# The opening modulation computed by quarters instead of by halves

## The reference, cut to what matters

```python
cond = jax.nn.silu(c)                                   # c: (1, 1024)
mod = (cond @ ada_w[0] + ada_b[0])[:, None, :]          # ada_w[0]: (1024, 6144)
sh1, sc1, g1, sh2, sc2, g2 = jnp.split(mod, 6, axis=-1)
h = rmsnorm(x, norm1_g[0]) * (1 + sc1) + sh1            # x: (1, 256, 1024)
proj = h @ w_in[0] + b_in[0]
```

## Time and profile before

| | us |
|---|---|
| three runs | 1454.43, 1455.65, 1456.05 (median 1455.65) |
| the profiled execution | 1453.79 |
| its span in the trace | 1452.0 |
| PE busy in the span | 1430.3 |
| POOL busy | 1211.7 |
| ACT busy | 756.5 |
| DVE busy | 722.8 |

### The profile page before, as it was taken

One profiled execution on the slowest core, in us unless ns is written; L12 is line 12 of the kernel. 1 busy time (PEld: TensorE's weight loads), 2 busy tenths in 40 slices (PEclk: granted clock), 3 DMA queues, 4 the chain that ended last, 5 costly groups with the idle time before them and its releaser, 6 DMA issues.

```text
span 1452.0 us, 21556 instructions
## 1 busy us (share of the span) xinstructions
PE 1430.3 (99%) x7600; PEld 1199.9 (83%) x7600; DVE 722.8 (50%) x1556; ACT 756.5 (52%) x1275; POOL 1211.7 (83%) x986
## 2 busy tenths in 40 slices
PE   7999999999999999999999999999999999999997
PEld 5898777799988987778888888878888888788886
DVE  7863654766643754754566303454650044655202
ACT  4435775644445345765644445574654345655442
POOL 3899989898888987559898897967999977789995
PEclk9999999999999999999999999999999999999999
DMA  9994557688975986337676565643656656446651
GB/s 361 402 357 159 192 170 227 232 305 314 315 263 161 399 314 219 110 102 232 216 244 205 185 206 164 191 154 131 191 201 196 221 163 188 132 163 200 195 199 56
DMA packets 149559, 313.35 MB, mean 216 GB/s; under 512 B 10934, under 2 KB 31818, under 8 KB 149451
## 3 DMA queue, kind: packets, MB, share of 16 engines
q1 hardware_dynamic: 147696, 310.62, 63.6%
q10 hardware_dynamic: 1756, 1.35, 0.3%
HBM read 310.87 MB, written 1.06 MB: 215 GB/s over the span
## 4 chain that ended last, share of the span: by engine, by line
PE 92%; DVE 4%; ACT 2%; POOL 1%; DMA 1%; issue 1%; SPq 0%; POOLq 0%; DVEq 0%; ACTq 0%
PE bank L814 58%; PE bank L859 12%; PE bank L860 8%; PE bank L857 5%; PE bank L1022 1%; PE bank L1006 1%; POOL lo_units L751 1%; PE bank L895 1%; PE bank L992 1%; DMA x_rows<-in_x 1%; PE bank L1109 1%; PE bank L1038 1%; PE bank L1074 1%; ACT hi_units L1402 1%; PE bank L1064 0%
## 5 line engine op out<-in xcount | busy, mean ns | idle before, releaser
L751 POOL TENSOR_TENSOR lo_units<-raw_units,hi_units 128x512 fp32r<-128x512 f32 (+3 forms) x928 | 1151.5, 1276 | 219.2 <-ACT hi_units L1402 218.0
L1402 ACT ACTIVATE hi_units<-raw_units 128x1024 fp32r<-128x1024 f32 (+1 forms) x470 | 482.7, 1030 | 410.9 <-PE bank L814 248.4
L814 PE MATMUL bank<-hi_units,turned 128*128 128x512 f32 (+3 forms) x1600 | 441.2, 390 | 1.7 <-DVE turned L1940 0.8
L814 PEld LDWEIGHTS bank<-hi_units,turned 128*128 128x128 f32 x1600 | 291.6, 189 | 53.3 <-DVE turned L1940 2.8
L860 PE MATMUL bank<-turned,lo_units 128*128 128x256 f32 x1024 | 288.0, 281 | 0.0
L814 PE MATMUL bank<-hi_units,turned_wide 128*128 128x512 f32 x992 | 274.6, 391 | 0.0
L859 PE MATMUL bank<-turned,hi_units 128*128 128x512 f32 x736 | 259.2, 397 | 0.0
L814 PE MATMUL bank<-lo_units,turned 128*128 128x512 f32 (+3 forms) x800 | 252.7, 383 | 0.8 <-POOL lo_units L751 0.5
L814 PEld LDWEIGHTS bank<-hi_units,turned_wide 128*128 128x128 f32 x992 | 185.3, 188 | 38.5 <-issue 0.5
L860 PEld LDWEIGHTS bank<-turned,lo_units 128*128 128x128 f32 x1024 | 194.3, 190 | 0.2
L814 PEld LDWEIGHTS bank<-lo_units,turned 128*128 128x128 f32 x800 | 149.7, 188 | 30.6 <-POOL lo_units L751 3.6
(11 more groups left out here) (266 smaller groups left out, 1290.9 us busy)
## 6 DMA issues: line engine op xcount, KB each, us to landing
ada_units<-in_ada_w SPq DMA_DIRECT2D x88, 512.0 KB, 7.7
raw_units<-in_w_ffn_tiles SPq DMA_DIRECT2D x72, 512.0 KB, 5.5
raw_units<-in_mlp_w_out SPq DMA_DIRECT2D x64, 512.0 KB, 3.3
raw_units<-in_mlp_w_tiles SPq DMA_DIRECT2D x56, 512.0 KB, 3.3
raw_units<-in_w_in SPq DMA_DIRECT2D x56, 458.0 KB, 9.8
raw_units<-in_w_in SPq DMA_DIRECT2D x48, 512.0 KB, 6.8
raw_units<-in_w_ffn_out SPq DMA_DIRECT2D x44, 512.0 KB, 3.5
raw_units<-in_moba_w_qkv SPq DMA_DIRECT2D x24, 512.0 KB, 3.7
```

What stands on the lines that cost most here:

```text
L751: pool.tensor_tensor(LO[:, s, b, 0:w], RAW[:, u["slot"], b, 0:w], HI_[:, s, b, 0:w].bitcast(F32), ALU.subtract).then_inc(lo_ready.sem, lo_ ...
L814: ins = pe.matmul(BANK[2 * c["pair"] + t][:, 0:w], (A[a] if A is BT else A[:, a])[:, part, t * P:(t + 1) * P], W[:, s, b, 0:w], start=(i = ...
L1402: act.activation(HI_[:, s, 0:n, 0:w], RAW[:, u["slot"], 0:n, 0:w], ACT.Copy)\
```

## The change

The host rearranges the first 2048 columns of `ada_w[0]` that are wanted into four quarters of 512: 256 columns of scale and the 256 of shift that belong to the same two tiles of h. Bias and gain come as columns from the host too (`first_columns`), in one small transfer on ACT's queue, so the two products that turned rows into columns are gone, and so are the memsets of `FIRST`. PE, ACT and DVE now work by quarter: sums of a quarter, its two operations for scale and shift on DVE, the application to one group of h on ACT (both tiles), rounded copy, remainder, and then unit q of c0 and unit q of c1. The last ada unit of quarters 0 and 3 is multiplied by PE, (0, 0, 3) and (0, 3, 3). The transfers of c and of the constants move from SPq to ACT's queue, x comes after two ada units instead of five, and weight units are mixed in among the ada units. `tables()` and `angles()` stand behind the fourth quarter, as they stood behind the second half. ACT rounds weight units only behind each quarter's copy.

```diff
-FIRST_BANK = {(0, 2): 0, (0, 0): 0, (0, 3): 0, (0, 1): 0}
-PE_UNITS = {(0, 3, 1)}
+N_FIRST = 4
+PE_UNITS = {(0, 0, 3), (0, 3, 3)}
+FIRST_BANK = {(0, q): 0 for q in range(N_FIRST)}
...
-    scale0, shift0, scale1, shift1 = first = [ada(0, c) for c in (2, 0, 3, 1)]
+    first = [ada(0, q) for q in range(N_FIRST)]
     chunks.extend(first)
-    stream.extend(scale0["units"] + shift0["units"])
+    sums = [u for c in first for u in c["units"]]
...
+            behind = {4: (c0, 0), 5: (c1, 0), 8: (c0, 1), 9: (c1, 1), 12: (c0, 2), 13: (c1, 2)}
+            for n, u in enumerate(sums):
+                stream.append(u)
+                if n in behind:
+                    c, i = behind[n]
+                    stream.append(c["units"][i])
+            stream.extend((c0["units"][3], c1["units"][3], vec(*vec0), vec(*vec1)))
...
-        sp.dma_start(COND, dram["c"].rearrange("b (p k) -> (b p) k", p=P)).then_inc(c_in, 16)
-        sp.dma_start(CON[:, 0:n_early], dram["constants"][:, 0:n_early]).then_inc(const_in, 16)
...
-                if (l, c, i) == (0, 0, 1):
+                if (l, c, i) == (0, 0, 2):
                     for t in range(NT):
                         sp.dma_start(X[:, t, :], dram["x"][0, t * P:(t + 1) * P, :]).then_inc(x_in[t], 16)
-                src = dram["ada_w"][l].rearrange("(p k) n -> p k n", p=P)[:, i * UNIT_K:(i + 1) * UNIT_K, c * CW:(c + 1) * CW]
+                if (l, c) in FIRST_BANK:
+                    src = dram["ada_first"][c][:, i * UNIT_K:(i + 1) * UNIT_K, :]
+                else:
+                    src = dram["ada_w"][l].rearrange("(p k) n -> p k n", p=P)[:, i * UNIT_K:(i + 1) * UNIT_K, c * CW:(c + 1) * CW]
...
+        def column_sums(q):
+
+            u = quarters[q]["units"][-1]
+            shared = (0, q, u["i"]) in PE_UNITS
+            pe.wait_ge(ada_used.sem, ada_used.at(quarters[q]["units"][-2 if shared else -1]["index"]))
             for j in range(4):
-                at = (KT if n >= 2 else 0) + 4 * half + j
-                pe.matmul(columns[:, at:at + 1], FIRST[0:1, n * CW + j * P:n * CW + (j + 1) * P], ONES[0:1, 0:1], start=False, stop=False)
-
-        def column_products(c, i):
-
-            u = c["units"][i]
-            at = (KT if c["key"][2] >= 2 else 0) + 4 * (c["key"][2] % 2)
-            pe.wait_ge(ada_in[u["home"]][u["slot"]], 16 * (u["turn"] + 1))
+                ins = pe.matmul(columns[:, 4 * q + j:4 * q + j + 1], MOD[:, q * CW + j * P:q * CW + (j + 1) * P], ONES[:, 0:1],
+                                start=j == 0, stop=j == 3 and not shared)
+            if not shared:
+                ins.then_inc(product.sem, product.mark(("columns", q)))
+                return
+            pe.wait_ge(ada_in[u["home"]][u["slot"]], 16)
             for k in range(UNIT_K):
                 for j in range(4):
-                    ins = pe.matmul(columns[:, at + j:at + j + 1], ada_raw(u)[:, k, j * P:(j + 1) * P], COND[:, i * UNIT_K + k:i * UNIT_K + k + 1],
-                                    start=False, stop=False)
+                    ins = pe.matmul(columns[:, 4 * q + j:4 * q + j + 1], ada_raw(u)[:, k, j * P:(j + 1) * P],
+                                    COND[:, KT - UNIT_K + k:KT - UNIT_K + k + 1], start=False, stop=(k, j) == (UNIT_K - 1, 3))
             ins.then_inc(ada_multiplied.sem, ada_multiplied.mark(u["index"]))
 
...
+        def keep_running(n, bank):
 
             for _ in range(n):
-                pe.matmul(BANK[3][:, :], con("ident"), ada_raw(scale0["units"][0])[:, 0, :], start=True, stop=True)
-
-        pe.wait_ge(ada_in[scale0["units"][0]["home"]][scale0["units"][0]["slot"]], 16)
-        keep_running(1)
-        pe.wait_ge(first_gain_in, 16)
-        gain_columns(0)
-        pe.wait_ge(first_bias_in, 16)
-        bias_columns(scale0)
-        keep_running(2)
-        column_sums(scale0)
+                pe.matmul(bank[:, :], con("ident"), ada_raw(quarters[0]["units"][0])[:, 0, :], start=True, stop=True)
+
+        first_unit = quarters[0]["units"][0]
+        pe.wait_ge(ada_in[first_unit["home"]][first_unit["slot"]], 16)
+        keep_running(4, BANK[3])
...
-                keep_running(1)
-                column_sums(shift0)
-                keep_running(2)
-                for i in (0, 1):
-                    pe.wait_ge(turned_lo.sem, turned_lo.at((tag, i)))
-                    unit(c0, i, HT)
-                turn(tag, O, range(4), 2, ready)
-                turn(tag, O, range(4), 3, ready)
-                pe.wait_ge(rows.sem, rows.at(("columns", 0)))
-                gain_columns(1)
-                column_products(scale1, 1)
-                unit(c1, 0, HT)
-                column_sums(scale1)
-                column_sums(shift1)
-                unit(c1, 1, HT)
-                for c in (c0, c1):
-                    for i in (2, 3):
-                        pe.wait_ge(turned_lo.sem, turned_lo.at((tag, i)))
-                        unit(c, i, HT)
+                keep_running(1, BANK[3])
+                column_sums(0)
+                keep_running(1, BANK[3])
+                for q in range(N_FIRST):
+                    pe.wait_ge(turned_lo.sem, turned_lo.at((tag, q)))
+                    unit(c0, q, HT)
+                    if q + 2 < N_FIRST:
+                        turn(tag, O, range(4), q + 2, ready)
+                    unit(c1, q, HT)
+                    if q + 1 < N_FIRST:
+                        column_sums(q + 1)
...
+        def first_hi(q):
+
+            act.wait_ge(rows.sem, rows.at(("columns", q)))
+            act.wait_ge(turned.sem, turned.at((("n1", 0), q)))
+            bank = BANK[(TQ, TP)[q % 2]]
+            for k in (0, 1):
+                part = bank[:, k * S:(k + 1) * S]
+                ins = act.activation(part, part, ACT.Identity, scale=GAINED[:, 2 * q + k:2 * q + k + 1], bias=BIASED[:, 4 * q + 2 + k:4 * q + 3 + k])
+            ins.then_inc(act_side.sem, act_side.mark(("whole", q)))
+            act.wait_ge(act_side.sem, act_side.at(("whole", q)))
+            act.activation(HT[:, 2 * q:2 * q + 2, 0, :], bank[:, :].rearrange("p (k s) -> p k s", k=2), ACT.Copy)\
+                .then_inc(turned_hi.sem, turned_hi.mark((("n1", 0), q)))
 
...
+        act.dma_start(COND, dram["c"].rearrange("b (p k) -> (b p) k", p=P)).then_inc(c_in, 16)
+        act.dma_start(CON[:, 0:n_early], dram["constants"][:, 0:n_early]).then_inc(const_in, 16)
+        act.wait_ge(c_in, 16)
+        act.activation(CT, COND, ACT.Tanh, scale=0.5).then_inc(act_side.sem, act_side.mark("cond"))
+        act.dma_start(NM[:, 0:3 * KT], dram["first_columns"]).then_inc(first_in, 16)
...
-        prep(2)
         for l in range(DEPTH):
             if l == 0:
-                first_hi(0)
-                prep(NH)
-                first_hi(1)
-                prep(NH + 3)
+                for q in range(N_FIRST):
+                    if q == N_FIRST - 1:
+                        prep(2 * q + 1)
+                    first_hi(q)
+                    prep(2 * q + 2)
...
+        def first_sum(q, kt):
+
+            u = by_key["ada", 0, q]["units"][kt // UNIT_K]
+            if (0, q, u["i"]) in PE_UNITS:
+                return
+            part, partial = ada_raw(u)[:, kt % UNIT_K, :], BANK[SB_[0]][:, :]
+            if kt % UNIT_K == 0:
+                dve.wait_ge(ada_in[u["home"]][u["slot"]], 16)
+                ada_done[0] += 1
+            if kt == 0:
+                ins = v.tensor_scalar(partial, part, COND[:, kt:kt + 1], None, ALU.mult)
+            else:
+                n = KT - (UNIT_K if (0, q, KT // UNIT_K - 1) in PE_UNITS else 0)
+                total = MOD[:, q * CW:(q + 1) * CW] if kt == n - 1 else partial
+                ins = v.scalar_tensor_tensor(total, part, COND[:, kt:kt + 1], partial, ALU.mult, ALU.add)
+            if kt % UNIT_K:
+                tell(ins, ada_used, u["index"])
+            else:
+                link(ins)
+
+        def first_columns(q):
+
+            dve.wait_ge(first_in, 16)
+            last = by_key["ada", 0, q]["units"][-1]
+            if (0, q, last["i"]) in PE_UNITS:
+                dve.wait_ge(ada_multiplied.sem, ada_multiplied.at(last["index"]))
+            else:
+                dve.wait_ge(product.sem, product.at(("columns", q)))
+            cols = slice(4 * q, 4 * q + 4)
+            link(v.tensor_tensor(BIASED[:, cols], BANK[SB_[1]][:, cols], FIRST_BIAS[:, cols], ALU.add))
+            say(v.scalar_tensor_tensor(GAINED[:, 2 * q:2 * q + 2], BIASED[:, 4 * q:4 * q + 2], 1.0, FIRST_GAIN[:, 2 * q:2 * q + 2], ALU.add, ALU.mult),
+                ("columns", q))
 
...
-        sums_upto(5)
+        for kt in range(4):
+            first_sum(0, kt)
         dve.wait_ge(act_side.sem, act_side.at(("root", ("n1", 0))))
         say(v.reciprocal(RR[:, 0:NT], RSTD), "inverse root")
-        sums_upto(8)
+        for kt in range(4, KT):
+            first_sum(0, kt)
         for l in range(DEPTH):
             if l == 0:
-                first_columns(0)
-                sums_upto(15)
```

(67 more changed lines are left out.)

42 lines of the change are left out of this document (2 added, 40 removed).

## The result

The changed kernel takes 1466.07 us (median of six runs, 1463.90 to 1467.73), the kernel before 1455.80: the ratio is 1.0068 with a 95% interval of 1.0056 to 1.0079, some 10 us slower. The profiled execution took 1467.73, with a span of 1465.9. The forecast was 1463.9 in a range of 1459.8 to 1469.5. Quarters are numbered 0 to 3 here, so the fourth quarter is quarter 3.

What follows compares the result with a forecast made beforehand. PE was taken to bound the kernel, so an opening delay reaches the end nearly whole. Unit 8 6.7 us later plus 1.5 for the clock is 8.2, on 1455.65: 1463.9 us, range 1459.8 to 1469.5.

Steps and rivals of the forecast that it cites:

- Rival (b): The delay is absorbed behind the opening, the transfers setting the pace: about 1455 us; chance 0.07.
- Start of the work: Opening: ada units issued 0.9 us earlier and x there at 9.3, so PE's first unit starts at 20.8, 4.0 earlier.
- The boundaries: Between quarters: nothing covers the chain from column sums to remainder, so PE idles 3.04 us, three times.
- Rival (c): Quarter boundaries: the chain behind the sums is covered, unit 8 starts 2.4 to 3.7 us earlier, 1452 to 1453; chance 0.04.
- break-even: Quarter boundaries: the kernel gets faster if a boundary costs PE under 0.8 us (6.7 / 3 saved off each).
- The products: PE's products of the last ada unit in quarters 0 and 3: twice 1.95 us of pure cost, DVE being ready anyway.
- The tables: Behind the fourth remainder: tables exposed, 6.4 us to unit 8 instead of 10.0, two operations slow beside POOL; unit 8 at 59.1.
- The clock: PE's granted clock falls at each boundary: 0.5 us lost in each of quarters 0 to 2, together 1.5; bounds 0 to 5.1.
- rival (a): Clock stays low longer, at the first sums and through each quarter: 6.7 plus 6 to 9 us, about 1469; chance 0.17.
- My bound: Upper bound of the clock term: the whole 3.4 us at half rate under dense work, 1.7 a quarter, 5.1 together.

Runs made afterwards that it cites:

- three of the experiments: Changed kernel with column sums between a quarter's two units (1454.99 us); that plus all sums by DVE (1452.62); changed kernel with three 458-column fillers per gap (1463.08).
- the second experiment: Changed kernel with the column sums of quarter q+1 put between c0's unit q and c1's unit q: 1454.99 us, ratio 0.9993 to the kernel before.
- dense gap: Changed kernel with three matmuls of 458 columns by zeros behind the column sums of quarters 1 to 3: 1463.08 us, ratio 1.0043 to the kernel before.
- small work in the gap: Changed kernel with 11 idle-filling matmuls of 54 columns behind the column sums of quarters 1 to 3: 1467.09 us, ratio 1.0067 to the kernel before.
- late angles: Sums by DVE, column sums between units, rounding ahead of scale; then angles() behind taking out c0's results, weight units 8 to 10 rounded before the sines: 1456.77 us, ratio 0.9995.

## Why the prediction was right

**Nothing behind the opening takes the loss up.** From the start of unit 8 to the end of the span it is 1399.6 us in the kernel before (1452.0 - 52.41), 1400.4 in the changed one (1465.9 - 65.54), and 1399.9, 1400.2 and 1400.9 in three of the experiments (1453.1 - 53.19, 1450.8 - 50.63, 1462.1 - 61.21). Rival (b), absorption, falls: over a range of 15 us in the start of unit 8 the rest differs by 1.3 us.

**Start of the work.** 20.8 was forecast, 20.91 measured. It is right in part by luck. The transposes began at 13.29 and not at 12.5, since PE was held by its fillers, which began at 7.02 and not near 4.9. From there to the sums it was 1.7 us and not 2.1, and the 12 products took 2.6 and not 3.0 (from 15.03 to 17.62, to the next instruction). The errors cancel.

**The boundaries.** The three waits are 3.15, 3.15 and 3.00 where 3.04 plus 0.2 was written, and moving the column sums gave back what the boundary took: shown by the second experiment. The raw sums were ready before, as written: in the changed kernel PE waited for none of them. Rival (c) needed the chain to be covered. It isn't in this kernel; in the second experiment, where it is, the waits are 0.55, 0.54 and 0.98 (the break-even had been put at 0.8) and the time is level with the kernel before, and with the products gone too it is faster.

**The products.** Twice 1.95 of pure cost was claimed; without them the time fell by 0.30% of 1456, about 4.4 us by the ratios and 4.2 by the medians. The rows give 1.8 for each of the two sets.

**The tables.** 6.4 us from the fourth remainder to unit 8 was forecast, by one slow operation for each POOL remainder. Where PE didn't cover it, it was 6.5 (44.16 to 50.63), 6.5 (46.71 to 53.19) and 6.5 (54.74 to 61.21). The rule of the Trainium skill ("SBUF — State Buffer", SBUF: two separate sides) on operations that lock each other out fits these rows: with POOL's two remainders left, two operations are slow, and six when POOL works on, as in the earlier trace rows.

**The clock, the term that was mis-sized.** I took 0.5 us for each of quarters 0, 1 and 2, the loss seen in the earlier trace rows, and nothing in quarter 3. The dense gap measures it. For quarters 1 to 3: 65.54 - 32.96 = 32.6 in the changed kernel and 61.21 - 33.59 = 27.6 there, 5.0. Quarter 0 lasted 12.05 (20.91 to 32.96), and quarter 1 of the dense gap, the same work at the full rate, 9.99 (33.59 to 43.58), another 2.1. Together 7.0 in this execution, against 1.5. The other terms stand: at the full rate the quarters take 9.99, 9.99 and 11.16 and the tables 6.47, which puts unit 8 at 20.91 + 37.6 = 58.5, where my sum had 59.1. The clock makes the rest of the way to 65.54.

So the profiled execution is rival (a), which had asked for 6 to 9 for the clock. By these (a) meant 1468.4 to 1471.4, so the stated range held the lower part of (a), not most of it as was written. Between the profiled executions the difference is 13.9 us where 8.2 was forecast. Between the medians it is 10.3, and there the dense gap gained 3.0 us, less than in the trace. That the median came out so near the forecast is luck in part: the profiled execution of the kernel before lies 2.0 us under its median, that of the changed kernel 1.7 over its own. The mean granted clock doesn't show why: it is 0.990 or 0.991 in each of the changed kernel's six executions, from the shortest to the longest. The cause stays open, since only one execution of each kernel has a trace.

Why the term was too small: the row that I took had PE idle for 1.06 and 1.42 us with matmuls of 512 columns between, its one low stretch lasted 3.4 us, and 2.2 us of that had passed, under sums, fillers and waiting, before dense work began. Here three of the four stretches last 6.8 us, and most of each lies under dense work (from 20.91, 44.13 and 57.66 on). My bound, 1.7 lost in a quarter, was the better price (7.0 / 4 is 1.8), but not for its reason. It had stretches of 3.4 in mind; they are longer, and part of each is covered by what PE would have waited for anyway: POOL's remainder at the first unit of a quarter, and the tables in quarter 3, where the dense gap shows a wait of 1.20 that the changed kernel doesn't have. The Trainium skill ("TensorE: Matmul & The Clock Gate", Part 1) calls the half rate the default that activity lifts. The rows agree, at 34 to 36 us in the changed kernel (0.50) and in the dense gap (1.00).

One argument against rival (a) was weak: that the small products at 30 to 34 us left the clock high. In the run with small work in the gap PE was occupied for 3.5 of 4.1 us (40.24 to 44.34) and the clock fell.

## What to carry to other kernels

When a stage is cut finer so that the first part can begin sooner, count the chain at each new boundary, and look in the bottleneck engine's own list for what lies between the instruction that starts the chain and the wait for its end. Here it was nothing, three times; one unit moved by one place between them was worth 11 us, with the clock. Idle time of TensorE is to be counted with the slower work behind it, and an engine's relief (the one-column products) is only worth what the relieved engine was late by. And an operation moved out of PE's way must be followed on every engine's list: the late angles freed unit 8 and held up ACT's transfers.

## What was not expected of the hardware

A transfer of 4 KB on ACT's queue, issued at 0.72 at the same moment as a 512 KB transfer on SPq, landed after 4.4 us; issued by SPq ahead of it, after 1.6. The constants (69 KB) took 5.4 and 2.0. In these two runs a small transfer issued ahead of the large ones landed sooner than one issued beside them, though the time of the kernel was the same.

Eleven matmuls of 54 columns, 2.7 us of PE's time in a gap of 3.3, left the clock to fall to 0.50; three of 458 columns, 2.55 us in the same gap, kept it at 1.00.
